# Filling TensorE's waits inside two routings of a mixture of experts with products of the identity

## The reference

```
logits = x @ router_w                                  # (tokens, 16)
probs  = softmax(logits); sel = probs + router_b
best group of 4 (by its two largest sel), then the top 2 experts inside it
wts    = probs of the two, divided by their sum
hid    = silu(x @ w_gate[e]) * (x @ w_up[e])           # 1024 -> 512, for the chosen experts
out    = sum over the chosen e of wts * (hid @ w_down[e])   # 512 -> 1024
x      = LayerNorm(alpha * x + out)
```

## Time and profile before

| | |
|---|---|
| median of 3 runs | 1082.03 us |
| all runs | 1083.13, 1073.86, 1082.03 us |
| the profiled execution, its own time | 1088.54 us |
| its span, first to last instruction | 1086.7 us |
| mean granted clock of TensorE | 0.882 |
| TensorE busy | 959.5 us, 88% of the span |
| weight loads of TensorE | 544.9 us, 50% |
| VectorE, GpSimd, ScalarE busy | 421.8, 240.2, 184.4 us |
| read from and written to the main memory | 261.5 and 18.0 MB, 257 GB/s over the span |
| chain that ended last | TensorE 69%, DMA 18%, VectorE 8%, ScalarE 2% |

### The profile page before, as it was taken

How to read it: one execution, slowest core, us unless ns; L and a number is a source line. 1 busy time by engine, 2 the same in 40 slices (tenths; PEclk the granted TensorE clock), 3 DMA queues, 4 the chain that set the end, 5 groups by cost and what they waited for, 6 DMA issues and landing times.

```text
span 1086.7 us, 11896 instructions
## 1 busy us (share of the span) xinstructions
PE 959.5 (88%) x4732; PEld 544.9 (50%) x4732; DVE 421.8 (39%) x851; ACT 184.4 (17%) x308; POOL 240.2 (22%) x339
## 2 busy tenths in 40 slices
PE   6999987999897499999989859989946999999991
PEld 5888867987333333333333359974413333333330
DVE  4799137622445511222223266621273211111126
ACT  0401212112002011111111152111131111111012
POOL 4679953201122141000000120000121000000000
PEclk9999988977588689999999975559976999999996
DMA  9457466002346849999999953353086899999962
GB/s 254 102 184 282 173 186 220 10 1 89 130 149 222 332 173 399 406 407 397 406 406 422 422 164 125 113 205 155 0 343 246 332 372 406 405 399 399 416 283 79
DMA packets 83576, 277.48 MB, mean 255 GB/s; under 512 B 25337, under 2 KB 44231, under 8 KB 60854
## 3 DMA queue, kind: packets, MB, share of 16 engines
q1 hardware_dynamic: 72474, 256.26, 61.6%
q10 hardware_dynamic: 8484, 16.09, 4.5%
q0 software_dynamic: 2560, 4.33, 1.4%
HBM read 261.49 MB, written 18.01 MB: 257 GB/s over the span
## 4 chain that ended last, share of the span: by engine, by line
PE 69%; DMA 18%; DVE 8%; ACT 2%; issue 1%; POOL 1%; SPq 0%; ACTq 0%; DVEq 0%; POOLq 0%
PE ps L1701 15%; DMA ring<-in_moe_w_up 15%; PE ps L318 11%; PE ps L1725 6%; PE ps L2364 5%; PE ps L742 3%; PE ps L1739 3%; PE ps L1680 2%; PE ps L2242 2%; PE ps L2227 2%; DMA ring<-s_out_mats 2%; PE ps L721 2%; PE ps L603 1%; PE ps L616 1%; PE ps L2240 1%
## 5 line engine op out<-in xcount | busy, mean ns | idle before, releaser
L1701 PE MATMUL ps<-ring,work 128*64 128x512 f32 x480 | 219.9, 610 | 12.4 <-DMA ring<-in_moe_w_up 10.8
L1702 PE MATMUL ps<-ring,work 128*64 128x512 f32 x480 | 220.0, 610 | 0.0
L1701 PEld LDWEIGHTS ps<-ring,work 128*64 128x64 f32 x480 | 64.1, 140 | 140.9 <-issue 122.8
L1781 DVE TENSOR_TENSOR work<-ps,work 64x512 f32<-64x512 f32 x32 | 33.8, 1055 | 222.4 <-ACT work L1752 222.4
L1725 PE MATMUL ps<-ring,work 128*64 128x512 f32 x248 | 113.0, 598 | 2.6 <-DVE work L1786 1.4
L318 PE MATMUL ps<-work,ring 128*128 128x264 f32 x512 | 115.2, 387 | 0.0
L1726 PE MATMUL ps<-ring,work 128*64 128x512 f32 x248 | 113.1, 598 | 0.0
L318 PEld LDWEIGHTS ps<-work,ring 128*128 128x128 f32 x512 | 96.8, 190 | 16.4
L1160 POOL TENSOR_TENSOR ring<-ring 128x512 f32<-128x512 f32 (+5 forms) x76 | 90.5, 1208 | 9.0 <-DVE ring L1156 5.7
L1802 POOL COPY work<-work 64x1 int32<-64x1 int32 x32 | 5.7, 180 | 331.5 <-PE ps L1680 292.7
L1791 DVE COPY work<-ps 64x512 f32<-64x512 f32 x32 | 22.2, 694 | 146.1 <-PE ps L1726 146.1
(11 more groups left out here) (481 smaller groups left out, 1336.3 us busy)
## 6 DMA issues: line engine op xcount, KB each, us to landing
ring<-in_moe_w_down SPq DMA_DIRECT2D x31, 2048.0 KB, 17.9
ring<-in_moe_w_gate SPq DMA_DIRECT2D x60, 1024.0 KB, 15.7
ring<-in_moe_w_up SPq DMA_DIRECT2D x60, 1024.0 KB, 18.2
ring<-in_w_in ACTq DMA_DIRECT2D x6, 2048.0 KB, 9.2
s_out_mats<-ring SPq DMA_DIRECT2D x4, 1280.0 KB, 4.7
ring<-in_w_in SPq DMA_DIRECT2D x2, 2048.0 KB, 10.3
s_in_mats<-ring SPq DMA_DIRECT2D x4, 1024.0 KB, 6.4
ring<-in_w_out SPq DMA_DIRECT2D x1, 4096.0 KB, 17.1
```

The lines of the kernel that those rows point to most:

```text
L1701: nc.tensor.matmul(ps[0:SLOT, 5, :], xgT[s][:, c], gate_w[slot][:, c], start=c == 0, stop=c == DC - 1)
L1702: last = nc.tensor.matmul(ps[SLOT:P, 5, :], xgT[s][:, c], up_w[slot][:, c], start=c == 0, stop=c == DC - 1)
L1781: nc.vector.tensor_tensor(hid[s][0:SLOT].rearrange("t (c p) -> t p c", c=4), strided(ps[SLOT:P, 5, :]), strided(sg[s][SLOT:P]), ALU.mult). ...
```

## The change

A function `keep_busy(bank, times)` issues `times` products of the identity matrix by the identity repeated four times (128x128 by 128x512), into one PSUM bank that holds nothing at that point. No instruction waits for them, and their result isn't read. They are issued on TensorE right before the waits of the routings: behind each tile's transposes (4 and 2 times in the first routing, 0 and 7 in the second), before the wait for `mask` (8), before that for `lists` (5), and behind the last product of the routing (2). Nothing is removed or moved.

```diff
+        def keep_busy(bank, times):
+
+            for _ in range(times):
+                nc.tensor.matmul(ps[:, bank, :], ident, ident.unsqueeze(1).to_broadcast([P, 4, P]), start=True, stop=True)
+
         def xT_pe(t, tag):
 
             for i in range(TT):
@@ -1403,6 +1408,7 @@
                     last = nc.tensor.transpose(bank4(xT_bank[i] + k // 4)[:, k % 4], xres[:, i, k * P:(k + 1) * P], ident)
                     if k % 4 == 3:
                         last.then_inc(*pe.done(f"{tag}xT{i}{k // 4}"))
+                keep_busy(0, {"n00": 4, "n01": 2, "n20": 0, "n21": 7}[f"{tag}{i}"])
 
         def xT_rest_pe(t, tag):
 
@@ -1438,12 +1444,14 @@
             for k in range(DC):
                 last = nc.tensor.matmul(ps[0:NS, 1, TT * NE:3 * NE], xT[:, k, SEQ:], router[:, k], start=k == 0, stop=k == DC - 1)
             last.then_inc(*pe.done(f"{tag}logits"))
+            keep_busy(0, 8)
             t.wait_ge(*dv.at(f"{tag}mask"))
             flat_mask = rt(9, 48)
 
             nc.tensor.matmul(ps[:, 1, 0:48], before, flat_mask, start=True, stop=True)
             nc.tensor.matmul(ps[:, 1, 48:96], ones, flat_mask, start=True, stop=True).then_inc(*pe.done(f"{tag}pos"))
 
+            keep_busy(0, 5)
             t.wait_ge(*dv.at(f"{tag}lists"))
             for n in range(6):
                 last = nc.tensor.matmul(ps[0:SLOT, 1, 128:128 + LISTS], at_slot[:, n], list_value[:, n], start=n == 0, stop=n == 5)
@@ -1454,6 +1462,7 @@
                     last = nc.tensor.matmul(ps[SLOT * half:SLOT * half + SLOT, 0, 0:2 * LISTS], at_slot[:, n],
                                             list_sel[:, n].rearrange("p a b -> p (a b)"), start=n == 0, stop=n == 5)
             last.then_inc(*pe.done(f"{tag}sel"))
+            keep_busy(2, 2)
```

## The result

The changed kernel takes 1089.32 us (median of 20 runs, 1080.97 to 1093.89) against 1081.71 us of the kernel before (20 runs, 1073.05 to 1094.14): ratio 1.0071, interval 1.0045 to 1.0098. Forecast were 1073 and a range up to 1081. A few executions of a kernel (the profiled one of small_hold01_p43 among them) are over 1.5% above its fastest, at a lower clock: ratios leave them out, medians and ranges hold all.

What follows compares the result with a forecast made beforehand. TensorE's low clock in the routings, a serial chain with VectorE and the gather, was taken as the bound. Gains 4.7 + 1.2 + 0.7 + 4.5 = 11.1 us, less 0.7 and 1.7, say 9 off 1082.03: 1073; range 1065 to 1081.

Steps and rivals of the forecast that it cites:

- The products fit into the waits: TensorE's routing pauses: added products at 0.87 us each all fit, leaving 0.4 to 1.6 us.
- The lower rival (3): Both routings: identity products don't hold the clock, take 1.65 us each and overrun; 17 us slower, 1099; chance 0.05.
- The router products: Both routings: 3.5 us at full clock, saving 3.1 and 1.6 us, all on the chain; 4.7 us.
- The position products nothing: Routing, after the mask: no gain, since VectorE's own work on the weights hides them.
- the list products 0.6 each: Both routings: VectorE's wait of 0.6 us for the list products disappears; 1.2 us together.
- The gather: Layer 0's token gather, issued some 3.7 us earlier, meets a weight load's tail; 0.7 us lost.
- some 2 us past the issue: Layer 0's gather: the weight load ends at 375 us, so it can't be held much longer than that.
- The sign named for it, a gather over 5 us: Profile of the changed kernel: a gather taking over 5 us would show the prediction wrong.
- off the chain: Second list products (selection) in the routing: no gain, since the gather ends last.
- The bounds of a landing, 2.9 and 7.5 us: Gather time: 2.9 us on idle transfer engines, 7.5 us median in the experts' stretch; delay up to 4.6 us.
- The gain reaches the end: Experts' weight stream: its start is set by TensorE's first four experts and moves with them, length unchanged.
- nothing else: Both routings: the change adds 21 and 22 identity products, with no wait, transfer or signal.

Runs made afterwards that it cites:

- small_hold01_p43: Changed kernel with routing products cut to 8 columns, expert loads waiting for the first gather in both layers, 43 cheap padding products up front: 1081.90 us, ratio 1.0032.
- after_p43: Changed kernel with 43 cheap products (8 columns of weights and data) ahead of TensorE's first work, no load made to wait: 1085.73 us, ratio 1.0063.
- small: Changed kernel with the same number of added products, each 8 columns instead of 512: median 1085.17 us, ratio 1.0045 to the kernel before.
- before_pad21: Kernel before with 21 products of 8 columns ahead of TensorE's first work; profiled once, not timed: 753.6 us from first transposes to end.
- hold01: Changed kernel with a load of expert 2's weights waiting for the first gather in each layer: median 1076.02 us, ratio 0.9962 to the kernel before.
- hold01_p43: Changed kernel with expert 2 loads waiting for the first gather in both layers and 43 cheap padding products up front: 1073.77 us against 1078.88, ratio 0.9955.

## Why the prediction was wrong, step by step

* **The products fit into the waits: right.** One takes 0.87 to 0.89 us (16 records in 7.13), none overran, and what was left over, 0.96 to 1.59 us, lies in the range given. The lower rival (3) that the identity doesn't hold the clock is out: 1.00 in both routings. The Trainium skill's rule on transposes ("TensorE: Matmul & The Clock Gate", Part 4) speaks of transpose mode only; ordinary products with the identity held 1.00 here.
* **The router products: right.** 3.63 us (3.5 said). VectorE's wait went from 5.1 and 3.7 us to 2.1 and 2.3: 3.0 and 1.4 against 3.1 and 1.6.
* **The position products nothing, the list products 0.6 each: right.** The gathers were issued 32.13 and 32.25 us after the first transposes instead of 35.89 and 34.48, so 3.8 and 2.2 us earlier; 3.7 and 2.2 were said.
* **The gather: wrong, and this is the step that failed.** I gave it "some 2 us past the issue" at most in layer 0, with 0.7 taken, and nothing at all in layer 1. It grew by 3.8 us (3.3 to 7.1) and 6.3 us (3.7 to 10.0). The sign named for it, a gather over 5 us, came in both layers. So the first experts began 0.4 and 4.1 us later than before, not some 3.2 and 2.7 earlier (3.1 + 0.6 + 0.15 less 0.7, and 1.6 + 0.6 + 0.5), and the pauses of 4.86 and 7.71 us let the clock fall again, with 8.13 and 9.43 us for the first expert's pairs. For layer 0 I took it that the gather is free once the load ends, some 2 us past the issue. After the change the transfer engines' share fell to 0.49 between 363 and 364 us, 2 to 3 us past the issue, rose once more to 0.58 between 365 and 366, and was at most 0.06 behind that, yet TensorE had to wait until 368.18. What held the gather in these last 4 to 5 us isn't shown. A share of 0.05, as in the last of the windows above, may be one of sixteen transfer engines still at work; that is a guess. Counted from the start of the weights the tokens were there after 39.6 us, before and after, as if the gather couldn't land earlier; but after_p43, the same code with padding, had them after 37.1 us. For layer 1 I had looked at what waits for TensorE's results on the chain, called the second list products "off the chain", and had not asked who else waits for them. SyncE's queue does, with 2 MB (its waits before, layer 1: us, times, longest):

```profile
SPq L1674 <- PE ps L1454: 21.2, 1, 21.2
```

* **The bounds of a landing, 2.9 and 7.5 us: enough for layer 0, not for layer 1,** whose gather of 10.0 us is above even the 9.7 of the earlier trace rows. A load issued 0.44 to 0.65 us behind the gather went with a gather of 7.3 to 10.0 us in four profiles (after, small, before_pad21, after_p43); one issued 1.61 us behind went with 3.7 us in one (before). The mechanism inside the transfer engines is not shown here. The Trainium skill ("DMA: Bandwidth & Descriptors", Queues, rings and completion order) says that a transfer's signal lands only after every earlier write of the same transfer engine, across queues, and that an engine takes a whole packet of one queue before it turns to another; either could hold up a gather; no run here tells them apart.
* **The gain reaches the end: right.** With the gathers held free, hold01 has 4.0 + 2.8 us in layer 0 and 3.0 + 1.7 in layer 1 up to the first expert's last pair, 11.5 us against 11.1 forecast. From the second routing's transposes to the end hold01_p43 took 291.1 us against 296.2, so layer 1's share is all there and the weight stream moved with TensorE. Over the whole kernel it is 0.77% by the ratios against the same kernel without activity, and 0.45% against before.
* **Missing altogether: the length of the list.** I wrote that the products add "nothing else". They add 172 instructions, of which 84 stand ahead of layer 0's branch, and there they bring a pause of 3.69 us and a low clock behind it, 5.6 us in the profile to the end of the combination (1.8 to 5.7 in the seven profiles).

So the gain from the clock exists and has about the forecast size, 6 to 8 us where 9 were said, and the result missed it because of what the prediction put at 0.7 us and at nothing. Without both disturbances the gain over the kernel before is 0.45% (0.14 to 0.76), some 5 us, half of the forecast. That hold01_p43's median of 1073.77 us meets the 1073 is luck: the kernel before ran at 1078.88 beside it. What remains open: why the kernel with tiny products, holds and padding is at 1.0032 and not at 1 (its interval holds both), and the share of each cause in the times. The two holds are worth 1.1%, the pause between nothing and its 5.6 us, and the times don't divide the 1.1% between the layers.

## What to carry to other kernels

When a change makes an engine faster on a chain, list everything that its signals release, the transfers above all, and look at what will then run beside the next transfer on the chain. A signal that is "off the chain" can start the load that holds it up. A small transfer that others wait for should be issued into an empty queue, and large loads made to wait until it has landed: here one wait in each layer, with the list moved, turned +0.7% into -0.5%. And before a change of the instruction count is judged by its time, try a padding or a control with the same count: the place of a branch in the list brought a pause of up to 3.7 us here, and in most profiles a low clock behind it.

## What the runs showed of the hardware that I had not expected

* The clock of a stretch of mixed small and large products has two outcomes. The output projection of layer 0 alternates four records with 32 rows and four with 128; at the lower level a group took 3.78 us for over 20 us on end, at the upper 1.98, in the same code. The first transposes of the first routing began between 327.2 and 342.7 us in the nine profiles in which no costly padding stood ahead of them. This alone spreads single executions over more than the change is worth.
* The pause at the branch came and went with the place of the list, 3.6 to 3.7 us at a shift of 84 or 128 instructions, 2.7 at 172, none at 0 and 256; each ended 2.65 to 2.76 us after a transfer of the instruction queue.
* A product of 8 columns costs 0.215 us a record with 128 columns of weights, 0.027 us (86 in 2.30 us) with 8, both at a granted clock of 1.00.
